# A hybrid encoder layer with 32 experts on one core: row-tiled scatter, one-row bias products, tokens gathered as rows

## What is computed

```python
hn = rms_norm(h, norm2_g)
top_v, top_i = top_k(hn @ w_router + b_router, 4); top_w = softmax(top_v)
for each expert e, for its tokens:
    hup = hn @ w_up[e] + b_up[e]                  # 1024 -> 2048
    glu = min(hup[:, 0::2], 7); lin = clip(hup[:, 1::2], -7, 7)
    act = glu * sigmoid(1.702 * glu) * (lin + 1)
    y[token] += top_w * (act @ w_down[e] + b_down[e])
out = h + y
```

## Time and profile before

| | |
|---|---|
| median of three executions | 1287.54 us |
| span of the profiled execution, first to last instruction | 1285.0 us |
| time around the span, against the median | 2.5 us |
| TensorE matmul busy | 1222.6 us, 95% |
| VectorE, ScalarE, GpSimd busy | 266.0, 181.0, 36.4 us |
| mean granted TensorE clock | 0.994 |
| bytes read from HBM | 432.72 MB |
| one expert block, start to start | 31.25 us, 31 times |

### The profile page before, as it was taken

The page is one execution under the profiler, slowest core; times in us unless marked ns, Lnnn a source line. Parts: engine busy times, 40 slices in busy tenths (PEclk is TensorE's granted clock), DMA queues, the critical chain, the costliest instruction groups (busy, mean ns, idle before and its releaser), DMA issues.

```text
span 1285.0 us, 16607 instructions
## 1 busy us (share of the span) xinstructions
PE 1222.6 (95%) x6090; PEld 636.9 (50%) x6090; DVE 266.0 (21%) x676; ACT 181.0 (14%) x377; POOL 36.4 (3%) x55
## 2 busy tenths in 40 slices
PE   6998999889999999999999999999999999999998
PEld 6786878754444444444444444444444444444443
DVE  7955135141111111111111111111111111111111
ACT  2132351021111111111111111111111111111110
POOL 4111000110000000000000000000000000000000
PEclk9999999999999999999999999999999999999999
DMA  7644339669999999999999996999999999999990
GB/s 169 196 131 70 99 102 350 257 245 361 402 403 399 401 405 399 404 404 400 410 399 407 401 407 275 401 398 405 407 398 407 406 407 405 391 405 400 404 403 34
DMA packets 121033, 435.83 MB, mean 339 GB/s; under 512 B 22800, under 2 KB 43328, under 8 KB 96384
## 3 DMA queue, kind: packets, MB, share of 16 engines
q1 hardware_dynamic: 120336, 433.65, 87.9%
q0 software_dynamic: 672, 1.86, 0.5%
HBM read 432.72 MB, written 1.57 MB: 338 GB/s over the span
## 4 chain that ended last, share of the span: by engine, by line
PE 92%; SPq 2%; ACT 2%; DMA 2%; issue 1%; DVE 1%; DVEq 0%; ACTq 0%
PE bank L901 34%; PE bank L932 18%; PE bank L863 9%; PE bank L854 9%; PE bank L602 4%; PE bank L797 4%; PE bank L582 3%; PE bank L556 2%; PE bank L826 2%; ACT arena L1146 2%; PE bank L770 1%; PE bank L627 1%; PE bank L782 1%; DMA arena<-in_w_out 1%; DMA arena<-in_w_in 1%
## 5 line engine op out<-in xcount | busy, mean ns | idle before, releaser
L901 PE MATMUL bank<-arena 128*64 128x512 f32 x2048 | 445.1, 592 | 0.0
L901 PEld LDWEIGHTS bank<-arena 128*64 128x64 f32 x2048 | 151.6, 137 | 287.4 <-issue 287.4
L932 PE MATMUL bank<-arena 128*64 128x512 f32 x1024 | 226.8, 595 | 27.7 <-ACT arena L1146 27.7
L1536 DVE TENSOR_SCALAR arena<-bank 128x256 f32<-128x256 f32 x64 | 26.9, 420 | 711.7 <-PE bank L901 711.7
L932 PEld LDWEIGHTS bank<-arena 128*64 128x64 f32 x1024 | 72.9, 137 | 160.9 <-issue 160.0
L854 PE MATMUL bank<-arena 128*128 128x128 f32 x1024 | 119.6, 275 | 1.4 <-DVE arena L1518 1.4
L863 PE MATMUL bank<-arena 128*128 128x512 f32 x256 | 118.4, 605 | 0.7 <-ACT arena L1149 0.7
L854 PEld LDWEIGHTS bank<-arena 128*128 128x128 f32 x1024 | 116.9, 192 | 1.5 <-DVE arena L1511 1.5
L1138 ACT ACTIVATE arena<-arena 128x512 f32<-128x512 f32 x32 | 20.2, 630 | 520.0 <-DVE arena L1537 520.0
L863 PEld LDWEIGHTS bank<-arena 128*128 128x128 f32 x256 | 46.0, 189 | 72.7 <-issue 71.1
L556 PE MATMUL bank<-arena 128*128 128x128 f32 (+1 forms) x322 | 51.5, 285 | 16.5 <-DVE arena L1182 8.8
(11 more groups left out here) (283 smaller groups left out, 586.5 us busy)
## 6 DMA issues: line engine op xcount, KB each, us to landing
arena<-in_w_up SPq DMA_DIRECT2D x192, 1024.0 KB, 8.0
arena<-in_w_down SPq DMA_DIRECT2D x128, 1024.0 KB, 11.0
arena<-in_w_up SPq DMA_DIRECT2D x128, 512.0 KB, 13.0
arena<-in_w_in SPq DMA_DIRECT2D x16, 1024.0 KB, 5.7
arena<-in_w_out SPq DMA_DIRECT2D x4, 1024.0 KB, 9.0
arena<-in_w_proj_ssm SPq DMA_DIRECT2D x8, 256.0 KB, 9.3
arena<-in_w_proj_att SPq DMA_DIRECT2D x2, 1024.0 KB, 11.4
arena<-in_x SPq DMA_DIRECT2D x2, 512.0 KB, 3.8
```

The source lines that it names most:

```text
L901: last = pe.matmul(B[n][64 * h:64 * h + 64, :], xg[:, k, :], up_w[parity][k][h][:, 512 * n:512 * n + 512], start=False, stop=(k == order[- ...
L932: last = pe.matmul(B[3][64 * n:64 * n + 64, :], actT[:, k % 4, k // 4, :], dn_w[parity][k // 2][:, k % 2, 512 * n:512 * n + 512], start=(k ...
L1536: TS(glu_t[:, 256 * n:256 * n + 256], v[:, 0, :], LIMIT, None, ALU.min)
```

## The change

It replaces four pieces of the expert block and moves two.

- **Scatter**: one tile `swT` (128 by 256) in place of `swT0` and `swT1`. Each product takes 64 rows only: rows 0 to 63 of `swT` and `y_s` for the first half of the outputs, rows 64 to 127 for the second. The zeros and one of the two copies on ScalarE go.
- **Up bias**: `bup` becomes 2 by 512 values in partition 0 and 2 by 512 in partition 64, loaded by two transfers of 4 KB instead of one of 8 KB. Each product takes one row (partition 0 or 64). The four products of block b+1 move from ahead of block b+1's up products to ahead of block b's down products.
- **Gather**: four products instead of 16. The selection (128 by 64) is now stationary and `hn` moves in pieces of 512. The result, tokens as rows in bank 2, is copied to `xrow` by ScalarE, turned by four transposes (`turn_rows`) and copied to `xg` in one copy.
- The activated values are transposed into bank 3 instead of bank 2, and TensorE waits for the copy of `swT` ahead of it. VectorE makes the selections when the row gather is done (`xr_ps`); the unweighted one is half as wide.
- GpSimd's zero fills of `bup`, `swT0` and `swT1` go, and SyncE waits for `out_ps` 3 in place of `bup_z`.

```diff
+            def load_bias(e):
+                v = b_up[bass.ds(e, 1), :].rearrange("o (h n c) -> o n h c", h=2, n=2)
+                for n in range(2):
+                    sp.dma_start(bup[64 * n:64 * n + 1], v[:, n]).then_inc(bup_in, 16)
-            sp.wait_ge(s["bup_z"], 1)
-            sp.dma_start(bup[0:1, :], b_up[0:1, :]).then_inc(bup_in, 16)
+            sp.wait_ge(s["out_ps"], 3)
+            load_bias(0)
...
                 sp.wait_ge(s["bup_used"], b)
-                sp.dma_start(bup[0:1, :], b_up[bass.ds(e, 1), :]).then_inc(bup_in, 16)
+                load_bias(e)
...
-                pe.wait_ge(bup_in, 16 * b + 16)
-                for n in range(2):
-                    for h in range(2):
-                        last = pe.matmul(B[n][64 * h:64 * h + 64, :], e0,
-                                         bup[:, D * h + 512 * n:D * h + 512 * n + 512],
+                pe.wait_ge(bup_in, 32 * b + 32)
+                for h in range(2):
+                    for n in range(2):
+                        r = 64 * n
+                        last = pe.matmul(B[n][64 * h:64 * h + 64, :], e0[r:r + 1, :], bup[r:r + 1, h, :],
                                          start=True, stop=False, skip_group_check=True)
...
+                for t in range(TT):
+                    for n in range(2):
+                        last = pe.matmul(B[2][64 * n:64 * n + 64, :], selg[:, t, :],
+                                         hn[:, t, 512 * n:512 * n + 512], start=(t == 0), stop=(t == TT - 1),
+                                         skip_group_check=True)
+                last.then_inc(s["xr_ps"], 1)
+            def turn_rows(nth):
+                pe.wait_ge(s["xrow"], nth)
+                transposes([(B[2][:, P * j:P * j + P], xrow[:, P * j:P * j + P]) for j in range(4)])\
+                    .then_inc(s["xg_ps"], 1)
...
-                    for n, sw in enumerate((swT0, swT1)):
-                        product = pe.matmul(B[4 + 2 * t + n][:, :], sw[:, t, :], y_s, start=False, stop=last,
-                                            skip_group_check=True)
+                    for n in range(2):
+                        r = slice(64 * n, 64 * n + 64)
+                        product = pe.matmul(B[4 + 2 * t + n][:, :], swT[r, t, :], y_s[r, :], start=False,
+                                            stop=last, skip_group_check=True)
...
-                if not first:
-                    pe.wait_ge(s["glu_sb"], b)
-                    up_bias(b)
-                pe.wait_ge(s["xg"], 2 * b + 2)
+                pe.wait_ge(s["xg"], b + 1)
...
                 if not last_block:
-                    gather(b + 2, b + 1)
+                    gather(b + 2)
                 pe.wait_ge(s["act"], b + 1)
-                if not last_block:
-                    pe.wait_ge(s["xg"], 2 * b + 3)
-                transposes([(B[2][:, P * j:P * j + P], act_s[:, P * j:P * j + P]) for j in range(4)])\
-                    .then_inc(s["aT2_ps"], 1)
+                pe.wait_ge(s["swT"], b + 1)
+                transposes([(B[3][:, P * j:P * j + P], act_s[:, P * j:P * j + P]) for j in range(4)])\
+                    .then_inc(s["aT2_ps"], 1)
+                if not last_block:
+                    pe.wait_ge(s["glu_sb"], b + 1)
+                    up_bias(b + 1)
+                    turn_rows(b + 2)
                 pe.wait_ge(s["aT2"], b + 1)
...
+            def gathered_rows(nth):
+                act.wait_ge(s["xr_ps"], nth)
+                act.activation(xrow, B[2][:, :], ACT.Copy).then_inc(s["xrow"], 1)
...
-                act.activation(swT0[0:64].rearrange("p a b -> p (a b)"), B[3][0:64, 0:2 * P], ACT.Copy)
-                act.activation(swT1[64:P].rearrange("p a b -> p (a b)"), B[3][64:P, 0:2 * P], ACT.Copy)\
+                act.activation(swT.rearrange("p a b -> p (a b)"), B[3][:, 0:2 * P], ACT.Copy)\
                     .then_inc(s["swT"], 1)
                 if not last_block:
+                    gathered_rows(b + 2)
+                act.wait_ge(s["aT2_ps"], b + 1)
+                act.activation(actT.rearrange("p a b c -> p (a b c)"), B[3][:, :], ACT.Copy)\
+                    .then_inc(s["aT2"], 1)
+                if not last_block:
                     gathered(b + 2)
```

More of the change, by code:

```diff
@@ L59 @@
  w_sb oT_ps o_sq o_ms o_var o_rs oT ps_ssm ps_att mixed h h_sq h_var h_rs hn hT_ps hT lg_ps top_e
- top_x gw rk_ps gT_ps gT bd_in bias_ps table_out table_in table bup_z sel xg_ps xg swt_ps swT glu_sb
+ top_x gw rk_ps gT_ps gT bd_in bias_ps table_out table_in table sel xr_ps xrow xg_ps xg swt_ps swT glu_sb
  sig act aT2_ps aT2 ysb summed up_used dn_used bup_used dsel fin fin_out wr_in g2_in loop_z u_turn
@@ L203, in mixer_and_experts @@
         hT = at(180, KT, TOK)
-        bup = at(120, 2 * D)
+        bup = at(120, 2, 512)
         bdn = at(128, D)
@@ L213, in mixer_and_experts @@
         selw = at(146, TT, P)
-        swT0, swT1 = at(147, TT, P), at(148, TT, P)
-        selg = at(149, TT, P)
+        swT = at(147, TT, P)
+        selg = at(149, TT, SLOTS)
         wr = at(188, KT, LC)
@@ L235, in mixer_and_experts @@
         g2b = at(156, D)
+        xrow = at(124, 4 * P)
         table_row = at(150, 3 * P).bitcast(I32)
@@ L490, in _ @@
                 link(last)
-            link(pool.memset(e0[0:1, :], 1.0))
+            for n in range(2):
+                last = pool.memset(e0[64 * n:64 * n + 1, :], 1.0)
+            link(last)
             pool.iota(iota, pattern=[[1, 5 * SLOTS]], base=0, channel_multiplier=0,
@@ L529, in _ @@
             pool.wait_ge(s["out_ps"], 3)
-            pool.memset(bup, 0.0).then_inc(s["bup_z"], 1)
             pool.memset(bdn, 0.0)
-            pool.memset(gwT, 0.0)
-            pool.memset(swT0, 0.0)
-            link(pool.memset(swT1, 0.0))
+            link(pool.memset(gwT, 0.0))
             pool.dma_start(bdn[0:E, :], a["b_down"][0]).then_inc(s["bd_in"], 16)
@@ L844, in _, with gather @@
             pe.matmul(o, ones, R2, start=False, stop=True).then_inc(s["rk_ps"], 1)
-            def gather(nth, turned=None):
+            def gather(nth):
                 pe.wait_ge(s["sel"], nth)
[L850 to L858, removed]
+                for t in range(TT):
[8 more added lines that the diff above has]
+                    .then_inc(s["xg_ps"], 1)
             def scatter(last=False):
                 for t in range(TT):
-                    for n, sw in enumerate((swT0, swT1)):
-                        product = pe.matmul(B[4 + 2 * t + n][:, :], sw[:, t, :], y_s, start=False, stop=last,
-                                            skip_group_check=True)
+                    for n in range(2):
+                        r = slice(64 * n, 64 * n + 64)
+                        product = pe.matmul(B[4 + 2 * t + n][:, :], swT[r, t, :], y_s[r, :], start=False,
+                                            stop=last, skip_group_check=True)
                         if last:
@@ L939, in _ @@
             gather(1)
+            turn_rows(1)
             expert_block(0, 0, first=True)
@@ L1126, in _ @@
                                bias=xs[:, t:t + 1], accum_out=xr[:, t:t + 1]).then_inc(s["top_x"], 1)
+            def gathered_rows(nth):
+                act.wait_ge(s["xr_ps"], nth)
+                act.activation(xrow, B[2][:, :], ACT.Copy).then_inc(s["xrow"], 1)
             def gathered(nth):
[L1130 to L1134, removed]
+                act.wait_ge(s["xg_ps"], nth)
+                act.activation(xg.rearrange("p (n j) c -> p j n c", n=2),
+                               B[2][:, :].rearrange("p (j n c) -> p j n c", j=4, n=2), ACT.Copy).then_inc(s["xg"], 1)
             def expert_block(b, last_block=False):
@@ L1139, in expert_block @@
                 act.wait_ge(s["swt_ps"], b + 1)
-                act.activation(swT0[0:64].rearrange("p a b -> p (a b)"), B[3][0:64, 0:2 * P], ACT.Copy)
-                act.activation(swT1[64:P].rearrange("p a b -> p (a b)"), B[3][64:P, 0:2 * P], ACT.Copy)\
+                act.activation(swT.rearrange("p a b -> p (a b)"), B[3][:, 0:2 * P], ACT.Copy)\
                     .then_inc(s["swT"], 1)
                 if not last_block:
+                    gathered_rows(b + 2)
[3 more added lines that the diff above has]
+                if not last_block:
                     gathered(b + 2)
-                act.wait_ge(s["aT2_ps"], b + 1)
-                act.activation(actT.rearrange("p a b c -> p (a b c)"), B[2][:, :], ACT.Copy)\
-                    .then_inc(s["aT2"], 1)
                 act.wait_ge(s["dn_used"], 4 * b + 4)
@@ L1151, in _ @@
             act.wait_ge(s["loop_z"], 1)
+            gathered_rows(1)
             gathered(1)
@@ L1514, in one_hot @@
             def one_hot(dst, e, first, weighted):
+                copies = 2 if weighted else 1
                 for t in range(TT):
-                    last = TS(dst[:, t, :].rearrange("p (d n) -> p d n", d=2),
```

(5 more changed lines are left out.)

4 lines of the change are left out of this document (removed).

## The result

The changed kernel takes 1239.68 us in the median (1237.82 to 1245.15, 4 runs), the kernel before beside it 1288.29. The ratio is 0.9625, with a 95% interval of 0.9599 to 0.9652: 3.75% faster. The forecast was 1228 us in a range of 1214 to 1262. The profiled execution has a span of 1236.1 us and a time of 1237.82, so 1.7 us lie around the span.

The account below looks back on a forecast made before the run. TensorE bounded the kernel at 31.26 us a block, transfers next at 30.25. Transfers from 316 us bring the last bias at 1184.7; 40.4 to the end and 2.5 around the span give 1227.6, forecast 1228 us, range 1214 to 1262.

Parts of the forecast that it names:

- The limit and its price: Expert loop: after the change transfers set the pace, 12.58 MB at 416 GB/s, 30.25 us a block.
- TensorE's parts: Sections of TensorE's expert block, with 0.25 us per change of shape: block 27.74 us, 3.51 less than before.
- rival 2: Scatter and bias: row tiles not side by side, about 1286 us (4 in 100); all in turn or 0.57 drains, 1312 (8).
- The place of the wait: Ahead of the bias products, before the down products: TensorE waits 2.5 us per block for the bias, after some blocks.
- Rival 4, the clock: After bias waits: clock lowered, TensorE's block 29.4 us, wait shorter, time the same; part of the forecast's case, no separate chance.
- the sum: Whole kernel: last bias at 1184.7 us plus 40.4 gives span 1225.1; with 2.5 around it 1227.6 us.
- The block of the transfers: Each expert block's loads: 12.58 MB at 416 GB/s take 30.25 us, counted for 29 whole blocks.
- block 16's hole: 10 us without traffic at block 16, where the load order changes; forecast to close, 10 us more if it stays.
- The unbroken run: Transfers from 316 us: 29 blocks and six up tiles without the queue running dry, last byte at 1208.4 us.
- The way from the last bias to the end: Kernel's end: last bias landed at 1184.7 us, then 40.4 us of TensorE work and tail, span end 1225.1.
- Rival 1: Expert loop: transfers keep up and TensorE sets the pace, 110 us less, 1177 us; 3 in 100.
- the lead: Loads ahead of TensorE: blocks of 27 to 28 us for the first five or so and again after block 16.

Follow-up runs that it names:

- Runs 2 and 3: Only half the rows of each w_down tile loaded from block 2 on: 2 in the changed kernel, 1162.28 us; 3 in the kernel before, 1287.34 us.
- run 8: Kernel before with the row-tiled scatter and the one-row bias products in their old place, gather unchanged: 1233.7 us, ratio 0.9584.
- Run 1: Kernel before with the row-tiled scatter alone, one copy of the selection on ScalarE: 1238.43 us, ratio 0.9616.
- run 4: Changed kernel with all bias rows issued by GpSimd on its own queue: 1231.53 us, ratio to the kernel before 0.957.

## Why the prediction was right, and where it was off

**The limit and its price** held. 12.58 MB at 416 GB/s was the step on which the forecast stood, and 415 came. Runs 2 and 3 show that this, and not TensorE, sets the time of the changed kernel, and run 8 shows the point at which it takes over. Run 1 has the same time with TensorE as its limit, so that the time is the same is no evidence for it.

**TensorE's parts** were sized well, each a little high: scatter 1.97 (1.92), transposes 0.47 (0.37), gather 1.97 (1.87), transposes 0.70 (0.59), bias 1.11 (1.02), turning 0.70 (0.59), block 27.74 (27.09). The surplus of a change of shape, taken as 0.25, is near 0.15: two column pairs are 1.72, the gather took 1.87. The upper end of 0.57, taken from the first bias with 2.29 us, was misread. A window over just these products in the kernel before has a clock of 0.82 (third column from the end):

```profile
273.27:275.56 2.29, 2.29 (x9) 0.58 (x9) 1.67 (x9) 0.34 (x3) 0.00 (x0) 0.82 0.47 122
```

So 0.18 x 2.29 = 0.41 of the 0.57 us is the clock, and 0.16 is left for the shape. The branch of rival 2 in which each change of shape costs 0.57 had no ground. Rival 2, that half-height products don't run side by side, is out by the 1.92 and the 1.02.

The Trainium skill, *TensorEngine Tiling (Array Packing)*, Key Properties, says that a change of mode drains TensorE. The trace agrees in that every section that follows another shape has a surplus; seven of them come to about 1 us a block here. No run isolates the drain from other small costs at such a border.

**The place of the wait** held too: at the bias, first in block 4 (0.54 us), gone after block 16 and back four blocks later, with blocks of 27.1 us in both free stretches. It was up to 3.29 us long instead of 2.5, since TensorE's block was shorter by 0.65 and the step of the transfers longer by 0.20 (below).

**Rival 4, the clock,** came true, and its working with it. The bias products of successive blocks in the kernel after (timeline of TensorE):

```profile
442.50 1.09 PE L804 MATMUL bank<-arena 1*64 1x512 f32 x8 [3.29 <-DMA arena<-in_b_up]
472.92 1.09 PE L804 MATMUL bank<-arena 1*64 1x512 f32 x8 [1.62 <-DMA arena<-in_b_up]
503.39 1.09 PE L804 MATMUL bank<-arena 1*64 1x512 f32 x8 [1.62 <-DMA arena<-in_b_up]
...
625.20 1.98 PE L804 MATMUL bank<-arena 1*64 1x512 f32 x8 [3.29 <-DMA arena<-in_b_up]
655.63 1.09 PE L804 MATMUL bank<-arena 1*64 1x512 f32 x8 [0.25 <-DMA arena<-in_b_up]
```

and windows behind the first two (PEclk is the third column from the end):

```profile
443.50:447.00 3.50, 3.50 (x16) 1.31 (x14) 0.00 (x0) 0.60 (x1) 0.00 (x0) 0.55 1.02 426
...
474.00:478.00 4.00, 4.00 (x16) 1.39 (x16) 0.00 (x0) 0.60 (x1) 0.00 (x0) 0.57 1.02 424
```

After each of these two waits most of the next 3.5 to 4 us are at 1.2 GHz. What TensorE loses there (1.6 to 1.7 us of work), it waits less the next time: 3.29, then 1.62, 1.62. The step from one bias to the next stays 30.42, 30.47 us. So in the middle of the loop the clock costs nothing, as forecast.

**What was 11.7 us off.** Forecast span 1225.1, measured 1236.1. The profiled run's 1237.82 is 10.2 over the 1227.6 of the sum, the median of four another 1.9.

*The block of the transfers* was the largest miss. It was 12.58 MB at 416 GB/s, 30.25 us. From 472.92 to 686.08 there are seven steps, 30.45 us each; per step that is 12.59 MB, with the bias, at 413.5 GB/s. 29 x 0.20 = 5.8 us. The view of the transfers for just this stretch, and for the one from the first issue after block 16's hole to the last weight:

```profile
DMA packets 17814, 88.58 MB, mean 416 GB/s; under 512 B 1603, under 2 KB 1603, under 8 KB 12387
...
DMA packets 37534, 187.04 MB, mean 413 GB/s; under 512 B 3370, under 2 KB 3370, under 8 KB 26010
```

In the first the engines move 416 GB/s, 88.58 / 7 = 12.65 MB a step, 0.5% more than a step's issues. The second shows that this is no extra traffic: in it SyncE issues 186.8 MB, and 187.04 are counted, 0.3 MB of which can have been queued before. So the bytes of the issues are right, and what a step needs is a little longer than bytes over the packets' mean rate. At the very end the rate falls over some 2 to 3 us and not at once, which would fit DMA engines that are not all equally far; which engine a packet belongs to the trace doesn't say, and the cause stays open. The windows from which 416 was read were short, too: in the changed kernel 1020 to 1042 us has 413 and 880 to 902 us has 419.

*The unbroken run* did not start at 316 and did not stay unbroken at block 16. Windows of the kernel after:

```profile
762.00:770.00 8.00, 8.00 (x40) 2.54 (x38) 0.00 (x0) 0.00 (x0) 0.00 (x0) 1.00 0.87 324
...
316.00:324.00 8.00, 8.00 (x41) 2.59 (x36) 0.00 (x0) 0.00 (x0) 0.00 (x0) 1.00 0.98 360
```

Against 416 GB/s the first loses 1.8 us and the second 1.1. The hole was forecast to close; it shrank from 10 us to this. SyncE could issue the next up tile only at 764.32, since TensorE had stood 3.29 us for the bias of block 16 and then run part of its down products at half clock (9.54 us instead of 7.02):

```profile
747.01 1.46 PE L804 MATMUL bank<-arena 1*64 1x512 f32 x8 [3.29 <-DMA arena<-in_b_up]
748.40 1.12 PE L562 MATMUL bank<-arena 128*128 128x128 f32 x4
749.45 9.54 PE L939 MATMUL bank<-arena 128*64 128x512 f32 x32
```

Here the clock does cost something, though no run separates it from the wait. Together these terms are 8.7 of the 9.2 us by which the last byte is late (forecast 1208.4). It comes in slice 24 of the 1.15 us slices from 1190 us on, near 1217.6:

```profile
GB/s 431 417 410 427 420 406 427 435 392 442 427 413 420 395 413 413 410 388 402 420 413 399 189 103 0 0 0 0 0 0 0 0 0 0 0 0 32 381 387 112
```

*The way from the last bias to the end.* The end hangs on the last bias, not on the last byte. The bias had landed at 1193.4, 8.7 us later than the 1184.7 of the forecast. From there it took 42.7 us instead of 40.4. The down products behind it took 8.42 us instead of 7.09, again behind a wait for the bias (1.65 us at 1193.45) and at a clock of 0.80 over 1195 to 1203 us. And from the end of the last down products to the end of the span 7.1 us passed, 7.5 before and 5.8 in the forecast, which took the scatter's whole 1.7 us off there. The scatter's share of the chain falls from 3.71 to 1.18 us, but VectorE's additions behind it stand on the chain for 2.5 us where there were 0.7. 8.7 + 2.3 = 11.0 us on the span.

The measured time lay in the range because the rate and the hole had been given their worse ends there. The single number had each at its best.

**Rival 1** (TensorE sets the pace, 1177 us) is what run 2 shows when the bytes are cut: 1162, with blocks of 27.1 instead of 27.7. With all the bytes TensorE does set the pace as long as the lead lasts, down to 29.70 us a block for the whole kernel (run 1). The forecast had the lead in it, as its first five or so free blocks, and for blocks as short as the changed kernel's that is about what it is worth. The ceiling of 435 GB/s that the Trainium skill, *DMA: Bandwidth & Descriptors*, gives in Specifications was reached over no long window here; 419 was the most over 22 us, 417 over 100 us.

## What to carry to other kernels

When the pacing engine and the transfers are 3% apart, work out the second limit before sizing a change to the first: bytes per round over the rate that a full queue shows. Take that rate from rounds that follow one another at the limit, or from windows of many rounds: a window of 22 us can be 1% off. A saving beyond the second limit still counts as long as the lead of the loads lasts (in run 1 over all 31 blocks, at 0.75 us a block under the limit). What goes beyond that is a wait, and only its place can still be chosen. Before two equal times are taken as one limit, look at what waits in each. Don't put a small, urgent load behind megabytes in an in-order queue; here that cost some 8 us, together with the stretches at the lower clock. The best version of the study is the change with its bias on a queue of its own, 1231.53 us; scatter and bias rows alone, 1233.7 us, do nearly as well with far less.

## What the runs showed of the hardware

- Products on the two row halves of the array run side by side in float32, as column halves do: four of them, 64 rows by 128 columns, moving 512, took 1.92 us, where four over 128 rows took 3.63.
- Four one-row products in the four quarters took 1.02 us, near the 0.86 of a single one.
- A queue that is hardly ever empty moved 415 GB/s on this core from 320 to 1205 us (runs 1 and 4, and 414 in the changed kernel). Rounds of 12.59 MB that followed one another at that limit took 30.45 us, 413.5 GB/s.
- One-row products ahead of the up products made these 0.15 us longer (13.88 instead of 13.73), so part of a change of shape is paid by the section behind it.
- A wait of 1.62 us of an engine otherwise always busy was followed by a stretch at 1.2 GHz like one of 3.29 us. 87 waits of at most 0.6 us (run 4) were followed by none, though they add up to more.
